# Moving three pieces of work in a one-core kernel: a table store, a scaling and a product

## What is computed

```python
zA, zB, zC, zD, zG = split(x @ w_in)
y = rwkv7_mix(zA, ...)            # per head: layernorm of y, * lnx_g + lnx_b, + bonus, then * g
gates = sigmoid(zG)
for n, yb in enumerate((yA, yB, yC, yD)):
    merged = merged + gates[:, :, n] * (yb @ w_branch[n])
x = layernorm(ALPHA * x + merged @ w_out)
x = layernorm(ALPHA * x + moe(x) + ple)
# second block: logits + bias_g[t5_bucket(distance)], masked to the window
```

## Time and profile before

| | us |
|---|---|
| median of 3 executions (1720.59 to 1722.74) | 1722.17 |
| the profiled execution, its own time | 1723.5 |
| span of the profiled execution, first to last instruction | 1721.7 |
| PE busy | 1692.8 (98%) |
| DVE busy | 605.9 (35%) |
| ACT busy | 271.5 (16%) |
| POOL busy | 130.6 (8%) |

### The profile page before, as it was taken

One profiled execution on the slowest core, in us unless ns is written; L12 is line 12 of the kernel. 1 busy time (PEld: TensorE's weight loads), 2 busy tenths in 40 slices (PEclk: granted clock), 3 DMA queues, 4 the chain that ended last, 5 costly groups with the idle time before them and its releaser, 6 DMA issues.

```text
span 1721.7 us, 25566 instructions
## 1 busy us (share of the span) xinstructions
PE 1692.8 (98%) x10669; PEld 1009.5 (59%) x10669; DVE 605.9 (35%) x1116; ACT 271.5 (16%) x477; POOL 130.6 (8%) x181
## 2 busy tenths in 40 slices
PE   9999999999999999999999999999999999999998
PEld 8787888889553333333434333333333337999995
DVE  4684467456341211111111111112111126454773
ACT  1323115001011111110101010101001112111231
POOL 1000000552000000000000000000000000005600
PEclk9999999999999999999999999999999999999999
DMA  8564332554979999999999999999999997443251
GB/s 320 190 258 166 147 123 100 166 167 185 378 319 423 406 428 428 427 429 428 428 429 428 426 429 427 427 430 427 426 430 427 427 416 297 161 178 117 99 191 48
DMA packets 61975, 540.60 MB, mean 314 GB/s; under 512 B 5192, under 2 KB 12136, under 8 KB 32452
## 3 DMA queue, kind: packets, MB, share of 16 engines
q1 hardware_dynamic: 56160, 528.42, 74.7%
q10 hardware_dynamic: 3956, 5.86, 1.2%
q0 software_dynamic: 1776, 5.10, 0.9%
HBM read 533.57 MB, written 5.78 MB: 313 GB/s over the span
## 4 chain that ended last, share of the span: by engine, by line
PE 92%; DMA 3%; DVE 2%; ACT 1%; issue 1%; SPq 0%; DVEq 0%; ACTq 0%
PE small L1654 24%; PE small L1693 13%; PE proj L1865 11%; PE proj L956 11%; PE proj L1630 3%; PE small L1596 3%; PE proj L1157 3%; PE small L1642 2%; PE small L1661 2%; PE small L976 2%; PE proj L965 2%; PE proj L1140 2%; PE small L1793 2%; PE small L2062 2%; PE small L1519 2%; DMA arena<-in_expert_w_down 1%
## 5 line engine op out<-in xcount | busy, mean ns | idle before, releaser
L1654 PE MATMUL small<-arena 128*64 128x512 f32 x2048 | 446.2, 593 | 2.3 <-DMA arena<-in_expert_w_gu 1.0
L1654 PEld LDWEIGHTS small<-arena 128*64 128x64 f32 x2048 | 151.5, 137 | 281.3 <-issue 276.0
L1693 PE MATMUL small<-arena 128*64 128x512 f32 x1024 | 227.0, 595 | 8.3 <-ACT arena L2288 7.4
L3024 DVE TENSOR_SCALAR arena<-small 128x512 f32<-128x512 f32 x32 | 22.1, 691 | 533.8 <-PE small L1661 533.8
L1865 PE MATMUL proj<-arena 128*128 128x128 f32 x1680 | 192.7, 276 | 0.0
L1865 PEld LDWEIGHTS proj<-arena 128*128 128x128 f32 x1680 | 189.4, 192 | 3.3 <-issue 2.5
L956 PE MATMUL proj<-arena 128*128 128x256 f32 x832 | 183.0, 380 | 0.0
L956 PEld LDWEIGHTS proj<-arena 128*128 128x128 f32 x832 | 157.1, 190 | 22.0 <-issue 0.5
L1693 PEld LDWEIGHTS small<-arena 128*64 128x64 f32 x1024 | 74.3, 137 | 139.5 <-issue 138.4
L852 POOL TENSOR_TENSOR arena<-arena 128x256 f32<-128x256 f32 x144 | 104.5, 759 | 159.3 <-PE proj L1865 98.8
L2283 ACT ACTIVATE arena<-arena 128x512 f32<-128x512 f32 x32 | 20.2, 630 | 490.3 <-DVE arena L3024 490.3
(11 more groups left out here) (461 smaller groups left out, 1618.3 us busy)
## 6 DMA issues: line engine op xcount, KB each, us to landing
arena<-in_expert_w_gu SPq DMA_DIRECT2D x128, 2048.0 KB, 19.3
arena<-in_expert_w_down SPq DMA_DIRECT2D x47, 2048.0 KB, 27.0
arena<-in_w_in_first SPq DMA_DIRECT2D x20, 2048.0 KB, 8.6
arena<-in_w_in SPq DMA_DIRECT2D x15, 2048.0 KB, 8.1
arena<-in_expert_w_down SPq DMA_DIRECT2D x17, 1536.0 KB, 29.1
arena<-in_w_ada SPq DMA_DIRECT2D x6, 2048.0 KB, 12.7
arena<-in_expert_w_down SPq DMA_DIRECT2D x17, 512.0 KB, 30.7
arena<-in_w_branch SPq DMA_DIRECT2D x4, 2048.0 KB, 8.6
```

Source lines behind the costliest of these rows:

```text
L1654: mm = pe.matmul(bank[CAP * half:CAP * half + CAP, :], XG[:, k % 4, k // 4, :], w[:, k % 4, n * D + half * W:n * D + half * W + W], start= ...
L1693: mm = pe.matmul(bank[CAP * half:CAP * half + CAP, :], h[:, m, u, :], w[:, half * W:half * W + W], start=u == 0 and m == 0, stop=u == 1 an ...
```

## The change

Three pieces of work are moved, none is added or removed. The numbers 0 to 3 of the gate units get names (GB0, GB1, GA0, GA1), which changes no instruction.

1. ACT: the DMA that stores the bias table, with its wait for `table_done`, goes from before the first `split_copy` of B to behind `early_gate(GB1)`.
2. DVE: the four `bonusA` instructions and the one of `gA` go from behind the additions of X5 to level 4, between the copies of X4 and the additions of D4.
3. PE: `y_turned(1)` goes ahead of `early_4(GA1)`. DVE: `y_normed(1)` goes ahead of `y_gated(0)`, and `c21(GA1)` goes behind `y_gated(1)`.

```diff
@@ tensor
             y_turned(0)
-            early_3(3)
-            early_4(3)
+            early_3(GA1)
             y_turned(1)
+            early_4(GA1)
             merge("A")
@@ scalar
                 out(f"A Kt {i}", Kt[:, i, :])
-            act.wait_ge(sig("table_done"), 1)
-            act.dma_start(scratch.rearrange("p h c -> h p c"), along(TAB, P)).then_inc(sig("table_stored"), 16)
...
+            early_gate(GB1)
+            act.wait_ge(sig("table_done"), 1)
+            act.dma_start(scratch.rearrange("p h c -> h p c"), along(TAB, P)).then_inc(sig("table_stored"), 16)
             act.wait_ge(sig("merged"), 3)
@@ vector
-                if l == 3:
-                    c22(0)
+                elif l == 3:
+                    c22(GB0)
+                else:
+                    for ct in range(4):
+                        do(STT(bonusA[:, ct, :], bonusA[:, ct, :], pv("rwkv_lnx_b", ct, ct + 1), gA[:, ct, :], ALU.add, ALU.mult))
+                    do(TTn(gA, gA, over(pv("rwkv_lnx_g"), T), ALU.mult))
                 for i in range(TT):
                     do(TTn(Dv[:, i], tiles(full(f"A D{l} {i}"), CH), Dv[:, i], ALU.add), "small_out")
...
                 do(TTn(X[:, 8 * i:8 * i + 8, :], tiles(full(f"A X5 {i}"), CH), along(c("eye64"), 8), ALU.add), "small_out")
-            for ct in range(4):
-                do(STT(bonusA[:, ct, :], bonusA[:, ct, :], pv("rwkv_lnx_b", ct, ct + 1), gA[:, ct, :], ALU.add, ALU.mult))
-            do(TTn(gA, gA, over(pv("rwkv_lnx_g"), T), ALU.mult))
             merge("B", False, (0,))
...
-            c22(3)
+            c22(GA1)
+            y_normed(1)
             y_gated(0)
-            y_normed(1)
-            c21(3)
             y_gated(1)
+            c21(GA1)
             merge("A", False)
```

More of the change, by code:

```diff
@@ L152 @@
 START = len(EARLY)
+GB0, GB1, GA0, GA1 = range(START)
 QKV = [f"{c}{g}" for g in range(GROUPS) for c in "QKV"]
@@ L875, in _ @@
             mask(2)
-            first_sums(0)
+            first_sums(GB0)
             mask(3)
-            last_sum(0)
+            last_sum(GB0)
             mask(4)
-            first_sums(1)
+            first_sums(GB1)
             mask(5)
-            last_sum(1)
+            last_sum(GB1)
             pool.wait_ge(sig("small_full"), small_no("Wb C 2") + 1)
@@ L885, in _ @@
             pool.dma_start(bcb, ins["ln1_b"][0].partition_broadcast(P)).then_inc(sig("ln1_loaded"), 16)
-            for u in range(2, START):
+            for u in (GA0, GA1):
                 first_sums(u)
@@ L1344, in _ @@
                 elif l == 3:
-                    early_5(0)
+                    early_5(GB0)
                 else:
-                    early_6(1)
-                    early_7(1)
+                    early_6(GB1)
+                    early_7(GB1)
                 if l == 1:
@@ L1358, in _ @@
                 elif l == 2:
-                    early_1(0)
-                    early_2(0)
+                    early_1(GB0)
+                    early_2(GB0)
                 elif l == 3:
-                    early_3(0)
-                    early_4(0)
+                    early_3(GB0)
+                    early_4(GB0)
                 else:
-                    early_5(1)
+                    early_5(GB1)
                 copied(f"D{l}", 1)
@@ L1372, in _ @@
                 elif l == 2:
-                    early_6(0)
-                    early_7(0)
+                    early_6(GB0)
+                    early_7(GB0)
                 elif l == 3:
-                    early_1(1)
-                    early_2(1)
-                else:
-                    early_3(1)
-                    early_4(1)
+                    early_1(GB1)
+                    early_2(GB1)
+                else:
+                    early_3(GB1)
+                    early_4(GB1)
             pe.wait_ge(sig("NTm_ready"), 4)
@@ L1482, in y_turned @@
                 mm.then_inc(sig("small_full"), 1)
-            early_1(2)
-            early_2(2)
+            early_1(GA0)
+            early_2(GA0)
             state(0)
-            early_6(2)
+            early_6(GA0)
             u_rows(1)
             y_of_states(0)
-            early_7(2)
+            early_7(GA0)
             state(1)
@@ L1493, in _ @@
             u_rows(2)
-            early_5(2)
+            early_5(GA0)
             state(2)
-            early_3(2)
-            early_4(2)
+            early_3(GA0)
+            early_4(GA0)
             u_rows(3)
             y_of_states(1)
-            early_1(3)
-            early_2(3)
+            early_1(GA1)
+            early_2(GA1)
             rows_of_y(1)
-            early_6(3)
-            early_7(3)
-            early_5(3)
+            early_6(GA1)
+            early_7(GA1)
+            early_5(GA1)
             y_turned(0)
-            early_3(3)
-            early_4(3)
+            early_3(GA1)
             y_turned(1)
+            early_4(GA1)
             merge("A")
@@ L2783, in _ @@
                 if l == 4:
-                    c11(1)
+                    c11(GB1)
                 x_copied(l)
@@ L2796, in _ @@
                 elif l == 2:
-                    c11(0)
+                    c11(GB0)
                 elif l == 3:
-                    c21(0)
+                    c21(GB0)
                 else:
-                    c22(1)
+                    c22(GB1)
                 for half in range(2):
@@ L2809, in _ @@
                     dve.nop().then_inc(sig("table_done"), 1)
-            c21(1)
+            c21(GB1)
             for i in range(TT):
                 do(TTn(X[:, 8 * i:8 * i + 8, :], tiles(full(f"A X5 {i}"), CH), along(c("eye64"), 8), ALU.add), "small_out")
-            for ct in range(4):
-                do(STT(bonusA[:, ct, :], bonusA[:, ct, :], pv("rwkv_lnx_b", ct, ct + 1), gA[:, ct, :], ALU.add, ALU.mult))
-            do(TTn(gA, gA, over(pv("rwkv_lnx_g"), T), ALU.mult))
             merge("B", False, (0,))
@@ L2894, in _ @@
             u_rows(2)
-            c22(2)
+            c22(GA0)
             state(2)
-            c21(2)
+            c21(GA0)
             u_rows(3)
@@ L2900, in _ @@
             y_of_states(1)
-            c11(3)
+            c11(GA1)
             y_normed(0)
```

43 lines of the change are left out of this document (21 added, 22 removed).

## The result

The kernel after takes 1724.92 us (median of 20 executions, 1719.15 to 1730.9) against 1721.13 us before (20 executions, 1718.61 to 1724.04): a ratio of 1.0027, 95% interval 1.0015 to 1.0039. (The ratio is between all executions, the medians alone differ by 3.8 us.) It is slower, where 5.5 us less were forecast, and 1.4 us above the upper end of the range.

What follows compares the result with a forecast made beforehand. PE was taken as the bound, nearly always busy, with gains carried to the end. -5.0 + 1.5 + 0.4 - 0.8 - 1.6 = -5.5 us took the median from 1722.17 to 1716.7, range 1714.8 to 1723.5.

Steps and rivals of the forecast that it cites:

- -5.0, stop and clock at level 4: At L1300, moving the store away removes PE's 3.24 us instruction stop and the slower clock behind it: 5.0 us gained.
- Rival 3: At level 4, "G A 0" alone holds the fetch, so the stop stays: -4 us, 1718.2; chance 0.07.
- +1.5, wait for D4's additions: At the head of L1311, the bonus on DVE delays D4's additions, so PE waits 1.1 to 1.8 us; 1.5 taken.
- the upper end: For D4's wait at L1311: the first bonus instruction can't run until POOL's masking is done, giving 1.8 us.
- +0.4, one fetch slightly late under the moved store: In PE's dense part beside the moved store, one instruction fetch comes slightly late: 0.4 us lost.
- rival 1: The stop moves: one fetch under the store 3 to 4 us late, dense part or expert loads; about 1720; chance 0.30.
- -0.8, AkT: At DT5, PE's wait for the masking of AkT (L2749) goes once the bonus is moved: 0.8 us gained.
- -1.6, end of A: Ahead of the merge of A, PE's wait for `y_gated(1)` goes, covered by `early_4`: 1.6 us gained.
- rival 2: Every block entered while the store runs takes 8 us: several stops and slow clock, 1726 to 1731; chance 0.13.
- the likeliest case: The forecast itself, with only one slightly late fetch (0.4 us) under the moved store: 1716.7 us; chance 0.45.

Runs made afterwards that it cites:

- x7: The kernel before with the first sixteen recorded matmuls of X0 done twice, 32 more PE instructions well ahead of level 4; the execution took 1721.21 us.
- x2: The kernel after with the table store back in its old place, the bonus and end-of-A changes kept; 1718.87 us, ratio 0.9988 to before.
- x5: The kernel after with 16 table copies instead of 128, HK loaded by eight DMAs spread over four units; 1718.74 us, ratio 0.9983 to before.
- x9: The kernel after with the first sixteen recorded matmuls of X0 done twice, 32 more PE instructions; 1723.86 us, ratio 1.0014 to before.
- x3: The kernel before with only the table store moved to its new place; 1728.97 us, ratio 1.0041 to before.

## Why the prediction was wrong

The sum was -5.0 + 1.5 + 0.4 - 0.8 - 1.6 = -5.5 us. Term by term:

- **-5.0, stop and clock at level 4: held in the traces, its size in the medians not shown.** L1301 runs through and `early_5` takes 2.05 us. Together with the waits for D4 and AkT the forecast put the head of the dense part 4.3 us earlier; it is 4.07 us earlier. The diagnosis (a block of 256 instructions fetched late) is borne out by x7. That the store's leaving cures it is seen from both sides: x2 keeps the store there and keeps the stop, and in after, beside "G A 0" alone, the packet of this block began at 350.85 us, 2 us after PE entered the block before. Rival 3 ("the stop at level 4 isn't the store's") is out. But the 3.24 us were one execution's: the stop was 2.06 us in x2 and 1.56 in x7. By the sum x2 and x5 should be 3.5 us apart (5.0 less 1.5); against the kernel before run beside each, their medians are 1.3 us apart and their intervals overlap.
- **+1.5, wait for D4's additions: 1.78, mechanism right, and it was the upper end.** The upper end supposed that the first bonus instruction can't run until POOL's masking ends, and that is what the trace of after shows:

```profile
349.87 2.36 POOL L848 TENSOR_TENSOR arena<-arena 128x1024 f32<-128x1024 f32 x1 [1.64 <-PE small L1290]
351.24 1.27 DVE L2795 SCALAR_TENSOR_TENSOR arena<-arena 128x256 f32<-128x256 f32 x1
L2795 DVE SCALAR_TENSOR_TENSOR arena<-arena x4: 831/834/1275, 351.2 to 354.3; 128x256 f32<-128x256 f32 x4
L853 POOL TENSOR_TENSOR arena<-arena x4: 907/908/910, 352.2 to 354.8; 128x256 f32<-128x256 f32 x4
```

The masking ended at 352.23 and the first of the four at 352.51, 0.28 us later, having taken 1.27 us where the others took 0.83. The others ran beside POOL's sums (L853), and they too lie one behind the other: POOL's first sum ended at 353.10, the second bonus instruction at 353.38, 0.28 us later again. The sums took 0.91 us each, where in before, with DVE idle beside them (352.3 to 355.0 us), they took 0.72. The Trainium skill says that such a pair excludes each other for the whole instruction ("SBUF — State Buffer", Who interferes with whom), and this trace agrees. The rest of the 1.78 is sizes: 5.5 us of bonus in a hole of 3.3.
- **+0.4, one fetch slightly late under the moved store: this is the step that failed.** It measured 4.87 us in the profile (3.28 of stop, 1.6 of slow clock), and half of the executions lost 6.9 us more, at a place that no trace shows. The text had both bounds, nothing and the full delay seen at level 4, and took a value by the lower one, on the ground that "the store by itself has its packets of 1.5 KB, and the one fetch that came very late stood behind packets of a 2 MB unit as well". That is a reason about sizes of packets without a row behind it, and the runs show the contrary: with hardly a packet of a 2 MB unit beside it (5 packets of q1 from 371 to 379 us), the store alone made the packet start 6.7 us after PE entered the block, as long as the store and "G A 0" together did at level 4 (6.4 us, 349.0 to 355.4). The prediction also misread its rows here. The last 42 matmuls of L1289 begin at 349.0 us, not 349.7, and the "8 to 9 us that it did at level 4" count the stop in: PE used that block up in 5.5 us (349.0 to 354.49), about as fast as the late one of after (5.7 us). So the shortness of the dense blocks, which the text feared, didn't decide it; the delay did, and its full size was on record. The evidence against rival 1, that fetches under the store brought no stop at levels 2 and 3, told little. By the same count PE entered a block at 339.8 us in both kernels and its packet began at 343.09 in before, under the store, and at 340.18 in after, without it: a delay of 3 us that a block of 9 us hid.
- **-0.8, AkT: held.** No wait on L2749 is left.
- **-1.6, end of A: held, at 1.5.** The merge follows `early_4` directly.

Put together, the lower group is rival 1 ("the stop moves", about 1720): with 4.87 in place of 0.4 and 1.78 in place of 1.5 the forecast span is 1716.2 + 4.5 + 0.3 = 1721.0, and 1720.8 was measured. The upper group has the times of rival 2 (1726 to 1731), which may be luck, for its mechanism, that every block entered while the store runs takes 8 us, is disproved for the executions with a trace: after has one stop and x9 none, under the same store. The Trainium skill's rule on turns of up to 64 descriptors ("DMA: Bandwidth & Descriptors", Queues, rings and completion order) spoke for these rivals. The trace is of its kind, in that a fetch from another queue waited for microseconds beside a queue of small packets, but no run here shows the size of a turn, and x9's timely fetches show that the wait isn't always taken.

The chances were off because the likeliest case and rival 1 differed by a single unknown with bounds of 0 and 5 us, and I gave the side without a row of its own 0.45 against 0.30 and 0.13.

## What to carry to other kernels

A long DMA that is moved away from where it delays an instruction fetch can delay one in its new place: look at every block that PE enters while the transfer runs, allow the full delay already on record, and count stop and slow clock both. Making the moved transfer shorter is what paid: an eighth of the store, its loads spread out, reached the forecast span in its profile and gained 3.2 us in the median. No run shortened it in its old place. And a removed wait is removed cover: the bonus was hidden only while the stop lasted, and splitting it into the holes that remain brought the last 2 us.

## What the runs showed of the hardware

- A stop for instructions comes in straight-line code, at a fixed count of instructions: 32 instructions more moved it by 32. In seven profiled executions of the kernels of after and x3 it was 2.7 to 3.4 us, at the same matmul of the code each time. PE ran again 2.3 to 2.5 us after the start of the late packet in before, after and x7.
- The same traffic beside a fetch doesn't fix its delay: 1178 and 1182 packets in 8 us, no block fetched in one kernel and two in the other, and the same block's packet 6.7 and 0.9 us after PE entered the block before it.
- After a stop of 3.3 us with PE idle, the granted clock stayed at 0.99 for 1.4 us of work and was then 0.50 for 3.4 us, which added half as much again to the loss.
- A DVE instruction with two inputs in SBUF and a POOL instruction that reads SBUF took turns: the first DVE one took 1.27 us and ended 0.28 us after POOL's, and POOL's took 0.91 us beside DVE against 0.72 with DVE idle.
- Eight DMAs of 384 KB and the unit behind them took SP 11.4 us to issue, one of 3 MB with the same rows and the unit behind it 5.6 us, most of it (5.26) shown at the unit.
- A profiled execution need not be like the others: none of nine was of a group that had 18 of 33 executions without the profiler.
